# Running sums of the stick-breaking attention: weights split in two rounded halves, fewer and other products

## What is computed

```python
z = einsum('bhqd,bhkd->bhqk', q_blk, kf) * scale
mask = key_pos < qpos
log1m = where(mask, log_sigmoid(-z), 0.0)
excl = cumsum(log1m, axis=3, reverse=True) - log1m
a = where(mask, exp(log_sigmoid(z) + excl), 0.0)
out = einsum('bhqk,bhkd->bhqd', a, vf)
```

## Time and profile before

| | us |
|---|---|
| median of 3 runs (lowest, highest) | 1160.28 (1159.47, 1160.7) |
| the profiled execution | 1162.27 |
| its span | 1160.4 |
| TensorE busy | 1049.6 (90%) |
| VectorE busy | 835.8 (72%) |
| ScalarE busy | 390.6 (34%) |

### The profile page before, as it was taken

The page is one execution under the profiler, slowest core; times in us unless marked ns, Lnnn a source line. Parts: engine busy times, 40 slices in busy tenths (PEclk is TensorE's granted clock), DMA queues, the critical chain, the costliest instruction groups (busy, mean ns, idle before and its releaser), DMA issues.

```text
span 1160.4 us, 11976 instructions
## 1 busy us (share of the span) xinstructions
PE 1049.6 (90%) x4108; PEld 664.9 (57%) x4108; DVE 835.8 (72%) x1744; ACT 390.6 (34%) x724; POOL 268.3 (23%) x261
## 2 busy tenths in 40 slices
PE   8999899998998778798877778889999999999998
PEld 6888464453454233244322222349878778888886
DVE  5887979778877768787787776765565496777743
ACT  7673312211220111320211012044765455444432
POOL 0001345434544334333433333400000000000000
PEclk9999999999999999999999999999999999999999
DMA  9847999999999999999999999977433454555540
GB/s 351 342 168 282 422 422 420 421 420 420 417 422 421 421 422 420 422 409 421 407 422 421 408 422 405 423 280 280 174 136 129 156 192 160 195 181 188 191 166 36
DMA packets 55531, 371.86 MB, mean 320 GB/s; under 512 B 6192, under 2 KB 7344, under 8 KB 12080
## 3 DMA queue, kind: packets, MB, share of 16 engines
q0 software_dynamic: 36864, 268.45, 56.0%
q1 hardware_dynamic: 18608, 102.65, 24.2%
HBM read 370.03 MB, written 1.05 MB: 320 GB/s over the span
## 4 chain that ended last, share of the span: by engine, by line
PE 55%; DMA 33%; DVE 7%; issue 3%; ACT 2%; POOL 1%; SPq 0%; DVEq 0%; POOLq 0%; ACTq 0%
DMA uv<-in_peer_uv,eidx 32%; PE bank L2187 13%; PE bank L1886 8%; PE bank L1888 7%; PE bank L1887 7%; PE bank L2361 6%; PE bank L1958 4%; DVE uv L1548 3%; PE bank L2360 3%; PE bank L1857 1%; POOL uv L721 1%; DVE diag L1562 1%; ACT w_hi L797 1%; DVE w_lo L1265 1%; DMA wraw<-in_in1a 1%
## 5 line engine op out<-in xcount | busy, mean ns | idle before, releaser
L2187 PE MATMUL bank<-uv,diag 128*128 128x512 f32 x1024 | 489.6, 606 | 96.9 <-DVE diag L1562 95.8
L1548 DVE SCALAR_TENSOR_TENSOR uv<-uv,xn 128x1024 f32<-128x1024 f32 x256 | 313.6, 1225 | 142.9 <-DMA uv<-in_peer_uv,eidx 141.3
L2187 PEld LDWEIGHTS bank<-uv,diag 128*128 128x128 f32 x1024 | 179.3, 190 | 371.4 <-issue 369.1
L721 POOL DMA_INDIRECT uv<-in_peer_uv,eidx x256 | 267.9, 1047 | 483.0 <-PE bank L2187 362.2
L1265 DVE TENSOR_TENSOR w_lo<-wraw,w_hi 128x2048 fp32r<-128x2048 f32 x69 | 157.8, 2290 | 102.3 <-ACT w_hi L797 102.2
L1008 ACT ACTIVATE chosen<-chosen 128x1 f32<-128x1 f32 x256 | 51.8, 203 | 514.1 <-DVE uv L1548 513.8
L797 ACT CAST w_hi<-wraw 128x2048 fp32r<-128x2048 f32 x69 | 131.5, 1908 | 125.6 <-PE bank L1888 63.2
L2361 PE MATMUL bank<-nT_both,w_hi 128*128 128x512 f32 x320 | 109.6, 396 | 0.0
L1562 DVE TENSOR_SCALAR diag<-const,chosen 128x128 f32<-128x128 f32 x256 | 89.4, 349 | 4.9 <-ACT chosen L1008 4.8
L2360 PE MATMUL bank<-nT_both,w_lo 128*128 128x256 f32 x280 | 78.1, 279 | 0.0
L2361 PEld LDWEIGHTS bank<-nT_both,w_hi 128*128 128x128 f32 x320 | 57.3, 188 | 10.8
(11 more groups left out here) (293 smaller groups left out, 1326.1 us busy)
## 6 DMA issues: line engine op xcount, KB each, us to landing
wraw<-in_ff_in SPq DMA_DIRECT2D x22, 1024.0 KB, 4.8
wraw<-in_ff_out SPq DMA_DIRECT2D x11, 1024.0 KB, 4.8
wraw<-in_query SPq DMA_DIRECT2D x4, 1024.0 KB, 5.1
uv<-in_peer_uv,eidx POOLq DMA_INDIRECT x256, 13.4
wraw<-in_in_q SPq DMA_DIRECT2D x2, 1024.0 KB, 9.7
wraw<-in_in_k SPq DMA_DIRECT2D x2, 1024.0 KB, 10.1
wraw<-in_pool_o SPq DMA_DIRECT2D x2, 1024.0 KB, 4.7
wraw<-in_sb_o SPq DMA_DIRECT2D x2, 1024.0 KB, 4.7
```

The costliest lines, as they stand in the source:

```text
L721: pool.indirect_dma_start(out=uv[:, RING_AT[n % RING], :], out_offset=None, in_=io["peer_uv"], in_offset=bass.IndirectOffsetOnAxis(ap=eidx ...
L1548: nc.vector.scalar_tensor_tensor(out=u, in0=u, scalar=1.0, in1=xn[:, head // PEER_HEADS, :], op0=ALU.mult, op1=ALU.mult, accum_out=hdot[he ...
L2187: mm = nc.tensor.matmul(acc[m][:, :], diag[:, n % RING, :], uv[:, RING_AT[n % RING], D + m * HALF:D + (m + 1) * HALF], start=(n % (ROWS // ...
```

## The change

The masked weights sp_l are split in two rounded halves: ScalarE copies them into l_hi, VectorE writes sp_l - l_hi into l_lo, both of the rounded type. The constants are copied once into `minus`, rounded (the triangle and the ones). Per head TensorE multiplies the triangle with columns 0:384 of both halves and the ones with columns 256:384 of both, 4 products in place of 3, now of rounded operands. On ScalarE `split_ahead(name)` stands ahead of the copy, so it is moved in front of the rest of the block's work where a pair has scores.

```diff
+        l_hi = place("l_hi", 138 * KB, [P, 2, 384], F32R)
+        l_lo = place("l_lo", 141 * KB, [P, 2, 384], F32R)
+        minus = place("minus", 144 * KB, [P, 2, P], F32R)
...
@@ ScalarE
+            nc.scalar.copy(minus[:, :, :], two(const[:, C0:C0 + 2 * P])).then_inc(minus_rounded, 1)
...
                     nc.scalar.activation(e_pair, e_pair, ACT.Ln, bias=1.0).then_inc(z_ln, 1)
+                    split_ahead(name)
+                    act.wait_ge(l_ready, z + 1)
+                    if z:
+                        act.wait_ge(cumulated, z)
+                    nc.scalar.copy(l_hi[:, :, :], sp_l[:, :, :]).then_inc(l_rounded, 1)
                 if attend is not None:
@@ VectorE
+                if p:
+                    dve.wait_ge(l_split, p)
                 nc.vector.tensor_tensor(sp_l[:, :, :], sp_e[:, :, :], spread(mask01, [[0, 2], [1, 384]]),
                                         ALU.mult).then_inc(l_ready, 1)
+                dve.wait_ge(l_rounded, p + 1)
+                nc.vector.tensor_tensor(l_lo[:, :, :], sp_l[:, :, :], l_hi[:, :, :].bitcast(F32), ALU.subtract).then_inc(l_split, 1)
@@ TensorE
-                    pe.wait_ge(l_ready, cum + 1)
+                    if not cum:
+                        pe.wait_ge(minus_rounded, 1)
+                    pe.wait_ge(l_split, cum + 1)
                     for a in range(2):
                         dst = bank[at("z", 2 * cum + a)[0]]
-                        nc.tensor.matmul(dst[:, 0:S], negtri, sp_l[:, a, 0:S], start=False, stop=False,
-                                         skip_group_check=True)
-                        nc.tensor.matmul(dst[:, P:S], negones, sp_l[:, a, S:384], start=False, stop=False,
-                                         skip_group_check=True)
-                        mm = nc.tensor.matmul(dst[:, S:384], negtri, sp_l[:, a, S:384], start=False, stop=True,
-                                              skip_group_check=True)
+                        for part in (l_hi, l_lo):
+                            nc.tensor.matmul(dst[:, 0:384], minus[:, 0, :], part[:, a, :], start=False, stop=False,
+                                             skip_group_check=True)
+                        for part in (l_hi, l_lo):
+                            mm = nc.tensor.matmul(dst[:, P:S], minus[:, 1, :], part[:, a, S:384], start=False,
+                                                  stop=part is l_lo, skip_group_check=True)
```

More of the change, by code:

```diff
@@ L506, in two_block_kernel @@
         l_ready = sem("l_ready")
+        minus_rounded = sem("minus_rounded")
+        l_rounded = sem("l_rounded")
+        l_split = sem("l_split")
         cumulated = sem("cumulated")
```

## The result

| | before | changed |
|---|---|---|
| median of 4 runs each (lowest to highest) | 1160.41 us (1159.47 to 1160.7) | 1167.94 us (1166.75 to 1169.38) |
| ratio, 95% interval | | 1.0061 [1.0049, 1.0073] |
| the profiled execution (its span) | 1162.27 (1160.4) | 1166.75 (1164.9) |
| first scores to cross attention ("the stage") | 58.33 us | 64.46 us |

The change costs 7.5 us. The profiled execution is the fastest of the four and 1.2 us under their median. The stage of the last row runs from pair 0's scores product to the cross attention's scores product right behind the last cumulation. These are its two ends, first in the kernel before, then in the changed one (timeline of TensorE: start, duration, line, tiles, the idle time before in brackets).

The account below looks back on a forecast made before the run. TensorE was taken as the bound, with ScalarE able to make it wait. Pauses less product savings gave +4.9 us, two dips +3.4: +8.3 on 1162.27, 1170.6, less 2.0 for the timed median, 1168.6 (range 1164.7 to 1170.4).

Parts of the forecast that it names:

- What bounds: In the edited stage TensorE is busy 29.00 of 29 us; ScalarE, with 23.21, is near enough to make it wait.
- The products: Cumulating products on TensorE: each pair of heads falls from 1.76 to 1.16 us, saving 0.6 (bounds 0.2 to 0.8).
- the signs: What would show it right: TensorE idle 3 to 4.5 us twice, Tanh 2.9 later, clock 0.5, cumulating groups 1.1 to 1.2.
- No wait for l_lo: Products at the tightest pair, pair 1: l_lo is ready at 833.1, TensorE arrives at 833.5, 0.4 us to spare.
- The moved cast costs nothing of its own: ScalarE behind Ln, block g0b: the 1.91 us weight cast fills the wait for VectorE's mask product, costing nothing.
- Tanh: Gates on ScalarE in blocks g0b and g1b: Tanh starts 2.95 us later behind Ln, with Ln about 0.2 earlier.
- The pauses: TensorE waits for gate banks that Tanh frees late, behind pairs 2 and 3: 4.2 and 3.3 us.
- The loss without clock: Net of both pauses and the products' savings at the end of the stage: +4.9 us (5.3 to 4.7).
- The clock: Behind both pauses TensorE's granted clock dips, 1.7 us of full-speed work lost each, 3.4 together.
- the rival with one dip: Both gate pauses come but only one clock dip: +6.6 us, 1166.9; chance 0.25.
- The faster rival: Gate banks come in time, so all four pairs' savings count: 2.4 us less, 1157.9; chance 0.05.
- longer dips: A gate pause so placed that the low clock lasts twice: up to 1.7 us more, 1170.3; chance 0.05.

Follow-up runs that it names:

- cast_back: The changed kernel with only the moved weight cast put back at the end of ScalarE's block, l_hi still ahead of Tanh: 1171.20 us, ratio 1.0089.
- no_idle_4_3: The changed kernel with 4 and 3 filler products on TensorE ahead of the two gate products that wait: 1165.46 us, ratio 1.0040.
- behind_gates: The changed kernel with l_hi copied behind Tanh and the weight cast last again on ScalarE: 1160.98 us, ratio 1.0000.
- on_vector: The changed kernel with l_hi copied by VectorE and ScalarE's list as before the change but for the constants: 1159.41 us, ratio 0.9985.
- att_first: on_vector, with VectorE also taking the earlier pair's weights out of their banks ahead of the weight split: 1158.54 us, ratio 0.9977.

## Why the prediction was right, and where it was off

The forecast was 1168.6 and slower, 8.3 over the time before; measured was 1167.94, 7.5 over. The 0.8 between them is 0.3 in the loss without clock and the rest in the clock's share. Step by step:

- **What bounds.** TensorE, with ScalarE near enough to make it wait: yes. TensorE's delay goes through to the end, with nothing lost on the way (the time behind the stage is equal within 0.1).
- **The products.** 0.6 per pair forecast, 0.67 measured. (The groups take 1.29 with the changes of operand kind at both ends, not the "1.1 to 1.2" of the signs; before it was 1.96 by the same measure.) 384 columns take 0.18 (forecast 0.17). The mis-sized term is the 128-column product, 0.12 forecast: the two of a head take 832.24 to 832.41, 0.17 together, 0.085 each. The Trainium skill (TensorE: Matmul & The Clock Gate, Back-to-back issue gap), with about 81 ns for that width, was nearer than the row that I took; the trace agrees with it as the mean of two, whose steps are 0.06 and 0.11.
- **No wait for l_lo:** none in any pair.
- **The moved cast costs nothing of its own:** right inside the block (0.28 idle behind it), shown by the equal 5.35 in cast_back. But I ended there. The step left out what the earlier cast does for VectorE's split of the same block and through it for att two blocks on, a gain of 1.4.
- **Tanh.** 2.95 later behind Ln: 2.93. Ln itself was to be 0.2 earlier and is 0.46 earlier (839.97 - 805.65 = 34.32, before 842.11 - 807.33 = 34.78): the weight split in front of att was to start when it did, and starts 0.23 earlier (27.85 for 28.08 behind the first scores). So Tanh came 2.47 later where I had 2.75. Block 6 was to start Tanh at 864.9 - 807.33 = 57.57; without a dip it did at 57.24.
- **The pauses.** 4.2 and 3.3 forecast, 4.00 and 3.58 measured, both by the weight loads. By the products they are 3.58 and 3.15, and it is with waits of products that I compared them: two measures, 0.4 apart.
- **The loss without clock.** 4.9 forecast, 4.59 in the stage, 4.8 in the runs of no_idle_4_3 (1165.46 - 1160.66).
- **The clock.** "I expect both to bring a dip" did not hold in the one execution that was profiled. I took two pauses of one execution for a rule by length; the last section shows that the same pause goes either way from one execution to the next. In this profile only the first brought a dip, so that execution, 1166.75, is the rival with one dip (1166.9 forecast). The price of a dip was right, 1.7 by the rows and 1.54 by the stage. Over the runs the dips cost about 2.4 against no_idle_4_3, or 7.5 - 4.6 = 2.9 against the stage without a dip; 3.4 was forecast. At 1.54 each that is between one and two dips, and the number in the runs without a profile stays open. So the direction and the pauses were reasoned; that the median came as near as 0.7 us hangs on how often the clock happened to fall.
- **The faster rival,** 1157.9: rightly out for the changed kernel, but I had its condition too simple. "If Tanh weren't held up" is what behind_gates and on_vector do, and they give 1.0000 and 0.9985. For all four pairs' savings the wait for att has to go as well. att_first has both and reaches it: 0.9977 of 1160.41 is 1157.7.

## What to carry to other kernels

A resource that frees an accumulator is part of TensorE's path even if its engine is busy a third of the time: before anything is put ahead of it, read how long TensorE has waited at that bank; 0.19 meant no slack, and every microsecond ahead of Tanh came back in full at each such bank. For the same reason products that get faster gain little by themselves where a bank's time hangs on the elementwise chain; here the copy on VectorE brought 1.6 of the 2.7 us, and the rest came when the weights of the earlier pair were taken ahead of the weight split. And an instruction that fills a wait may still be doing a job for another engine: ask who reads its result before calling its place free.

## What was unexpected of the hardware

- **The same pause brings a dip in one execution and none in the next.** The pauses of the earlier trace rows lie in code that no kernel here changes, and all twelve profiled executions have them, within 0.05. In the kernel before, the clock fell after the one of 2.70 and not after 3.02. The changed kernel had it the other way round (timeline of TensorE, then stretches; at 386 the clock is 1.00, at 428 it is 0.50, and 426 to 434 has the whole dip):

```profile
384.08 1.96 PE L2203 MATMUL bank<-uv,diag 128*128 128x512 f32 x4 [2.72 <-DVE diag L1574]
...
427.57 8.49 PE L2203 MATMUL bank<-uv,diag 128*128 128x512 f32 x12 [3.02 <-DVE diag L1574]
```

```profile
386.00:387.00 1.00, 0.41 (x2) 0.30 (x2) 1.00 (x9) 0.99 (x2) 0.00 (x0) 1.00 1.07 442
428.00:429.00 1.00, 1.00 (x2) 0.38 (x2) 0.00 (x0) 0.99 (x3) 0.00 (x0) 0.50 0.96 401
426.00:434.00 8.00, 6.36 (x8) 2.37 (x9) 6.04 (x21) 3.58 (x7) 0.94 (x1) 0.57 1.01 422
```

  Over the twelve it fell behind the pause of 2.7 in 8, behind that of 3.0 in 8, and behind one of 2.14 near 738 us in 5. At the gates, by the products' waits: after 2.48, 3.15, 3.58, 3.88, 4.32 and 5.00 us, not after 2.70 and 3.15, and never after 1.6 or less. At the gates such a fall costs the same each time: 1.70 or 1.71 us of lost work in its rows. Elsewhere it can cost double: behind the pause of 3.0 us the low clock lasted about 6.8 us in five of the eight cases (3.41 or 3.42 lost by the rows; 0.57 over the 8 us above), which is the mechanism of the rival "longer dips", though it didn't come at the gates. The fall can also start inside the pause (in the changed kernel the row 426:427 already has 0.79, and TensorE starts at 427.57). What decides in a given execution stays open. For a forecast from these rows, a pause of 2.1 to 3.2 us is a chance of a dip and not a dip; the four longer ones, 3.58 to 5.00, all had one, but each was seen only once.
- **Two narrow rounded products right behind each other** start 0.06 apart, a third of the 0.18 for three times the columns, though each has a weight load in the trace; the step from the second to the next wide product is 0.11.
- **VectorE's copy of 768 columns into the rounded type** takes 0.56, less than ScalarE's 0.83 and than VectorE's own passes with two inputs (0.96), as on_vector's timeline shows:

```profile
844.31 0.56 DVE L1675 CAST l_hi<-sp_l 128x768 fp32r<-128x768 f32 x1
```
